# RWKV head pairs: one signal for both heads' copies, weight passes moved from the pairs' fronts into their levels, decay work in other places, and attention's norm sums later

## The chip, the cores and the metric

The kernel runs on one core of one Trainium2 chip. The metric is the device time of one execution in microseconds (us). Before the change it is 2789.9 us, the median of three runs (2789.7, 2789.9 and 2792.98).

## What is computed

A first block (mixers and a feed-forward, not touched here) and then two layers of a hybrid block on 512 tokens of width 1024, all in float32. Each layer is

```
h = rms(x) * g1;  proj = h @ w_in
o_a = sliding_window_attention(rms(q), rms(k), v)     # per head norms
o_b = rwkv7_time_mix(...)                             # 8 heads of 64
o_c = retention(...)
x = x + (g0*o_a@W + g1*o_b@W + g2*o_c@W) @ w_out
x = x + (silu(h2 @ w_gate) * (h2 @ w_up)) @ w_down
```

The RWKV part is the recurrence

```
S = S * w_t + (S a_t) b_t + v_t k_t ;   y_t = S r_t
y = groupnorm(y) * g + b ; y = (y + bonus) * gate
```

with decays `w = exp(-exp(-0.5) * sigmoid(...))`. The kernel computes it in chunks of 64 tokens: inside a chunk a triangular 64x64 system is solved by doubling (one start and five **levels**), and between chunks the state S is carried in eight steps.

## The kernel before, in words

**Weights.** Every large product runs in three passes, since the weights and activations are split into a high and a low half that TensorE takes exactly: `w_hi*xg_hi`, `w_hi*xg_lo`, `w_lo*xg_hi`. One **slot** is one output tile of 128 columns: 8 blocks times 3 = 24 **passes** (128x128 by 128x512) into one of two accumulators, `acc[0]` and `acc[1]`. SyncE loads each slot's raw weights (512 KB) into `raw[s]`; GpSimd rounds them to `w_hi` (line 348, the **high part**) and subtracts to `w_lo` (line 352, the **low part**). GpSimd may write `w_hi[s]` only when pass 16 of the slot before on the same side has been read (`hi_done`), and `w_lo[s]` only after its pass 24 (`slot_done`). VectorE scales a finished accumulator by `rstd` and frees it (`take`).

**A layer's order.** Seven pairs of slots for RWKV; then four **head pairs** j = 0 to 3 (`rwkv_pair`), in which TensorE mixes RWKV's small products with the passes of four slots of the retention projection (96 passes each, given out by `fill(k)`); then three pairs of slots for attention's q, k and v with their norm sums (`head_sums`); then retention and attention themselves among the slots of the output products. The order is written out by hand on every engine: each engine is one queue, and semaphores (`after`, `say`) tie them. `say` on VectorE is a drain and a semaphore increment.

**One head pair** on TensorE: the **front** (32 passes with `variance(j-1)` in between, the `centre` products and transposes after `kh`, 8 passes, then after `ops` the two score products with `eM` and `kp` and transposes, 10 passes), then five levels, each of two **halves**: `X*TL` (32 small products), passes, a wait for `yi` and `gev`, `G*Y` (32 small products), passes, a wait for `xt`. After that the products `au`, `tq`, `dd`, `y0`, and the **tail**, eight state steps that go back and forth with VectorE. VectorE in a half: the two heads p = 0, 1 are copied one after the other (`Y` by an add with the identity, line 1055; `X` by a transpose, line 1626), and each copy is followed by its own `say`:

```
for p in range(2):
    after("y", j, 2 * (lev - 1) + p + 1, 10)
    tt(rw["Y"][:, p], ...)
    say("yi")
```

although TensorE waits for both, and gives both in one increment of 2. VectorE's front: norms, the exponentials' products (`bon`, `kp`, `AR`, `a`, `Dl`, `eM`), then `gated(j-1)` (three operations of the output of the pair before, lines 1535 to 1540), then `say("ops")`, `halves(j-1)` (the split of that output into y1_hi and y1_lo, which says `done`), a take, and the masked scores `SCB`. The next pair's decays are worked into the levels: the scan (line 1514) in level 2 after the transposes, its follow-up in level 3, the key factors in level 5. ScalarE copies G (`swapped`), and in levels 2 to 4 makes the next pair's sigmoids, exponentials and `to_end`. GpSimd masks `TL` (line 440) once a level and does the high and low part of side 0 before level 1 and of side 1 before level 3.

**Attention's norm sums.** TensorE runs `head_sums` of a pair of query tiles between slot 0 and slot 1 of the pair of slots after it, and those of the keys, with four transposes, right after the last slot; it waits there for the squares (line 1690) and then for the roots, before retention's first `rotate`.

## Time and profile before

| | before |
|---|---|
| median of 3 runs | 2789.9 us |
| the profiled execution's own time | 2790.91 us |
| its span, first to last instruction | 2789.1 us |
| mean granted TensorE clock | 0.986 |
| TensorE matmul busy | 94% of the span |
| VectorE, GpSimd, ScalarE busy | 53%, 53%, 23% |
| the two RWKV stretches (four head pairs each) | 786.8 to 1011.7 us and 1828 to 2053 us |

How to read it: the times are of one profiled execution; a matmul's end is modelled, so that a row of passes overlaps the next row a little. In the rows of the timeline the columns are start in us, duration in us, engine, line, operation, output<-inputs, shape and how many instructions were merged; in square brackets stands the idle time of the engine ahead of it and who ended it. PE is TensorE, DVE VectorE, ACT ScalarE, POOL GpSimd.

### The profile page before, as it was taken

Reading aid. Unit: us, or ns where it says so; the run is one execution under the profiler, and the core shown is the slowest. Engines: PE = TensorE matmul, PEld = TensorE weight load, DVE = VectorE, ACT = ScalarE, POOL = GpSimd, SP = SyncE. Lnnn points to the kernel's source line nnn. Section 1 sums busy time; section 2 is a strip of 40 time slices with the busy share of each in tenths; the row PEclk is TensorE's granted clock in tenths of the full one; section 3 lists DMA queues with packets and bytes.
Section 4 is the critical chain, followed back from the end, with each engine's and each line's share of the span. In section 5 each row is a group of like instructions: output and inputs, shape, how many; then the busy total and the mean of one; then the engine's idle time right before and its main releaser. Section 6 shows DMA issues by size and latency. Waiting matters only on the chain.

```text
span 2789.1 us, 47713 instructions
## 1 busy us (share of the span) xinstructions
PE 2634.2 (94%) x16458; PEld 2052.5 (74%) x16458; DVE 1465.7 (53%) x2075; ACT 627.9 (23%) x1143; POOL 1476.9 (53%) x945
## 2 busy tenths in 40 slices
PE   7878999998999899999999999999899989999999
PEld 5656888876766667777788887766667777788887
DVE  5766747364556646773342524456637764442424
ACT  2323000023223313440200002223323440200002
POOL 4554665665544343445666566644444446666665
PEclk9989999999999999999999999999999999999999
DMA  4212333323211121222233333311121223333333
GB/s 145 69 31 78 96 91 97 90 85 101 83 54 47 40 78 57 69 69 81 93 96 92 93 96 111 91 47 49 38 85 57 61 69 90 95 94 92 97 90 98
DMA packets 72727, 222.69 MB, mean 80 GB/s; under 512 B 9344, under 2 KB 12544, under 8 KB 72576
## 3 DMA queue, kind: packets, MB, share of 16 engines
q1 hardware_dynamic: 72576, 220.63, 26.1%
q8 instruction: 100, 1.64, 0.3%
q14 instruction: 51, 0.42, 0.1%
HBM read 218.50 MB, written 2.10 MB: 79 GB/s over the span
## 4 chain that ended last, share of the span: by engine, by line
PE 80%; DVE 10%; issue 4%; DVEq 3%; ACT 1%; DMA 1%; POOL 1%; ACTq 0%; SPq 0%; POOLq 0%
PE acc L464 70%; PE bank L464 8%; DVE rw_X L1626 1%; DVE rw_Y L1055 1%; DVEq L1499 1%; DVE an_mx L1800 1%; DMA raw<-in_w_pg 1%; PE bank L1021 1%; DVE y_lo L1055 0%; DVE an_mx L1055 0%; POOL w_lo L352 0%; DVE rw_SCK L1055 0%; DVE mixed L1055 0%; DVE rw_Dl L1055 0%; DVE an_s L1797 0%
## 5 line engine op out<-in xcount | busy, mean ns | idle before, releaser
L352 POOL TENSOR_TENSOR w_lo<-raw,w_hi 128x1024 fp32r<-128x1024 f32 (+3 forms) x438 | 959.3, 2190 | 300.4 <-PE acc L464 282.8
L348 POOL TENSOR_SCALAR w_hi<-raw 128x1024 fp32r<-128x1024 f32 (+3 forms) x438 | 427.5, 976 | 767.4 <-PE acc L464 645.0
L464 PE MATMUL acc<-xg_hi,w_hi 128*128 128x512 f32 x2224 | 601.9, 407 | 53.4 <-issue 16.0
L464 PE MATMUL acc<-xg_hi,w_lo 128*128 128x512 f32 x2224 | 588.3, 399 | 0.0
L464 PE MATMUL acc<-xg_lo,w_hi 128*128 128x512 f32 x2224 | 587.1, 400 | 0.0
L464 PEld LDWEIGHTS acc<-xg_hi,w_hi 128*128 128x128 f32 x2224 | 416.3, 190 | 174.6 <-issue 80.1
L464 PEld LDWEIGHTS acc<-xg_lo,w_hi 128*128 128x128 f32 x2224 | 419.8, 190 | 102.2 <-issue 1.5
L464 PEld LDWEIGHTS acc<-xg_hi,w_lo 128*128 128x128 f32 x2224 | 417.1, 188 | 101.7 <-issue 1.7
L1845 ACT ACTIVATE ffn_act<-ffn_t 128x512 f32<-128x512 f32 x100 | 63.3, 633 | 812.8 <-DVEq L1115 619.5
L1055 DVE TENSOR_TENSOR x<-x,acc 128x512 f32<-128x512 f32 x104 | 71.3, 688 | 318.4 <-PE acc L464 317.9
L464 PE MATMUL acc<-hid_hi,w_hi 128*128 128x512 f32 x656 | 182.8, 396 | 3.7 <-POOL w_lo L352 1.6
L464 PE MATMUL acc<-hid_hi,w_lo 128*128 128x512 f32 x656 | 182.0, 395 | 0.0
L464 PE MATMUL acc<-hid_lo,w_hi 128*128 128x512 f32 x656 | 181.9, 395 | 0.0
L464 PEld LDWEIGHTS acc<-hid_hi,w_hi 128*128 128x128 f32 x656 | 123.1, 188 | 37.4 <-issue 6.9
L464 PEld LDWEIGHTS acc<-hid_hi,w_lo 128*128 128x128 f32 x656 | 123.2, 188 | 29.9
L464 PEld LDWEIGHTS acc<-hid_lo,w_hi 128*128 128x128 f32 x656 | 123.2, 188 | 29.5
L1055 DVE TENSOR_TENSOR ffn_sq<-acc,rstd 128x512 f32<-128x512 f32 x44 | 30.4, 691 | 212.4 <-PE acc L464 212.4
L1055 DVE TENSOR_TENSOR ffn_t<-acc,rstd 128x512 f32<-128x512 f32 x100 | 69.2, 692 | 136.8 <-PE acc L464 119.4
L1862 ACT ACT_TABLE_LOAD x96 | 123.2, 1283 | 4.6 <-issue 1.7
L440 POOL TENSOR_TENSOR rw_TL<-rw_SCB,lev 128x512 f32<-128x512 f32 x40 | 51.1, 1277 | 97.0 <-DVEq L1499 56.3
L1055 DVE TENSOR_TENSOR ffn_h<-ffn_act,ffn_sq 128x512 f32<-128x512 f32 x44 | 96.0, 2182 | 11.5 <-issue 11.5
L464 PE MATMUL acc<-y_hi,w_hi 128*128 128x512 f32 x256 | 77.9, 427 | 17.9 <-issue 9.9
(342 smaller groups left out, 2738.9 us busy)
## 6 DMA issues: line engine op xcount, KB each, us to landing
raw<-in_w_up SPq DMA_DIRECT2D x132, 512.0 KB, 3.6
raw<-in_w_down SPq DMA_DIRECT2D x48, 512.0 KB, 3.6
raw<-in_w_gate SPq DMA_DIRECT2D x48, 512.0 KB, 3.6
raw<-in_w_ret SPq DMA_DIRECT2D x32, 512.0 KB, 3.6
raw<-in_w_rw SPq DMA_DIRECT2D x28, 512.0 KB, 3.6
raw<-in_w_o SPq DMA_DIRECT2D x48, 256.0 KB, 2.7
raw<-in_w_in SPq DMA_DIRECT2D x18, 512.0 KB, 3.6
raw<-in_w_down SPq DMA_DIRECT2D x24, 384.0 KB, 3.0
```

What stands on the lines that cost most here:

```text
L348: nc.gpsimd.tensor_scalar(w_hi[:, s, 0:n], raw[:, s, 0:n], 1.0, 0.0, ALU.mult, ALU.add).then_inc(w_half[s], 1)
L352: nc.gpsimd.tensor_tensor(w_lo[:, s, 0:n], raw[:, s, 0:n], bits(w_hi[:, s, 0:n]), ALU.subtract).then_inc(w_split[s], 1)
L440: nc.gpsimd.tensor_tensor(rw["TL"][:, lev % 2].rearrange("p h n t -> p (h n) t"), tl, K["lev"][:, lev:lev + 1, :].to_broadcast([P, 8, CH]) ...
L464: return nc.tensor.matmul(o, a, b, start=first, stop=last, skip_group_check=shared)
L1021: last = nc.tensor.transpose(bank[2 * p + j // 2][:, (2 * (j % 2) + b) * P:(2 * (j % 2) + b + 1) * P], an["s"][:, p, j, b * P:(b + 1) * P] ...
L1055: return v.tensor_tensor(o, a, b, op)
L1499: dve.drain()
L1626: v.transpose(rw["X"][:, p].rearrange("p n t -> p (n t)"), bank[3 + p][:, 0:T // 2])
L1800: v.tensor_reduce(an["mx"][:, hs], an["s"][:, p], AX.X, ALU.max)
L1845: return nc.scalar.activation(o, i, f, **kw)
L1862: nc.scalar.preload_act_table_set(name)
```

## The change

1. **One signal for both heads' copies.** In each level VectorE waits once, copies both heads and says `yi` by 2, and the same for `xt`.
2. **Passes.** TensorE's `fill` before `variance` goes from 24 to 14, the next from 8 to 10, the 8 ahead of `ops` go, and the 10 (8 in the last pair) ahead of level 1 become 14. The levels give out 5 per half where they gave 4; `au`, `tq` and the ones behind get one more each.
3. **Front.** `say("ops")` stands ahead of `gated(j-1)`; `gated` writes back to SBUF and says a new `gd`, for which TensorE waits ahead of the AR transposes; the gate product goes to bank 2. The split moves: its high half into level 3, its low half (with `done`) into level 4. `take(0, 0)` moves behind `g1`.
4. **Decays.** The sigmoid is written to SBUF (`eM`) instead of bank 0; the scan reads it there and moves from level 2 to level 5; its follow-up and the last two key steps move behind `auev`; ScalarE's exponentials and `to_end` move behind `keys`. `lora` and the sigmoids go from level 2 to 3, the product `w` from level 1 to 2, the key scores are split around level 1's transposes.
5. **GpSimd.** High and low part of side 0 no longer stand together ahead of level 1: the low part moves ahead of level 3's `TL`, side 1's high part ahead of level 4's, its low part ahead of level 5's.
6. **Attention.** The query sums come a slot pair later, the key sums and transposes inside the first slot of the output stage (after 10 of its passes), retention's value transposes behind that slot; waits for `s4 root` and `s3 z` ahead of them fall away.

The core of the diff:

```diff
 # GpSimd
-                    split_pair((DC, DC), I + 2 * j + 1, range(1))
+                    high_part(0, I + 2 * j + 1, DC * P)
                     for lev in range(1, 6):
                         if lev == 3:
-                            split_pair((DC, DC), I + 2 * j + 1, range(1, 2))
+                            low_part(0, I + 2 * j + 1, DC * P)
+                        elif lev == 4:
+                            high_part(1, I + 2 * j + 1, DC * P)
+                        elif lev == 5:
+                            low_part(1, I + 2 * j + 1, DC * P)
...
 # TensorE, rwkv_pair
-                    fill(24)
+                    fill(14)
                     if j > 0:
                         variance(j - 1)
-                    fill(8)
+                    fill(10)
                     after("kh", j, 1, 1)
...
-                    fill(8)
+                    if j > 0:
+                        after("yroot", j - 1, 1, 1)
                     after("ops", j, 1, 1)
...
                     if j > 0:
-                        after("done", j - 1, 1, 1)
+                        after("gd", j - 1, 1, 1)
...
-                    fill(10 if j < 3 else 8)
+                    fill(14)
...
                         last.then_inc(s2["y"], 2)
-                        if lev == 2 and j < 3:
-                            fill(1)
-                            after("wev", j, 1, 1)
-                            lora(j + 1)
-                        else:
-                            fill(4)
+                        if lev == 2:
+                            fill(3)
+                            after("scev", j, 4, 4)
+                            ...
+                            last.then_inc(s2["w"], 1)
+                        elif lev == 3 and j < 3:
+                            fill(2)
+                            after("wev", j, 1, 1)
+                            lora(j + 1)
+                        else:
+                            fill(5)
+                        after("gev", j, 2 * lev - 1, 11)
                         after("yi", j, 2 * lev, 10)
...
                         last.then_inc(s2["g"], 2)
-                        fill(4)
+                        fill(5)
...
-                    if j < 3:
-                        after("L", j + 1, 1, 1)
...
-                    fill(3 if j < 3 else 2)
+                    fill(4 if j < 3 else 2)
...
-                    fill(1)
+                    fill(2 if j < 3 else 1)
...
-                    fill(3 if j < 3 else 1)
+                    fill(4 if j < 3 else 2)
...
 # TensorE, attention and the output stage
+                slot(0, I, xg, full)
+                slot(1, I, xg, full)
+                variance(3)
+                slot(0, I + 1, xg, full)
+                slot(1, I + 1, xg, full)
+                query_sums(0)
+                slot(0, I + 2, xg, full)
+                after("done", 3, 1, 1)
+                query_sums(1)
+                slot(1, I + 2, xg, full)
...
-                    slot(0, F, xg, full)
+                    if n == 0:
+                        part(0, F, 0, 10)
+                        key_sums()
+                        part(0, F, 10, 24)
+                        values(0)
+                    else:
+                        slot(0, F, xg, full)
...
 # VectorE, rwkv_pair
                     tt(Dl, ra, Dl)
                     tt(eM, ra, eM)
+                    say("ops")
                     if j > 0:
                         gated(j - 1)
-                    say("ops")
-                    if j > 0:
-                        halves(j - 1)
-                    take(0, 0)
...
                     say("g1")
+                    take(0, 0)
                     for lev in range(1, 6):
+                        after("y", j, 2 * lev, 10)
                         for p in range(2):
-                            after("y", j, 2 * (lev - 1) + p + 1, 10)
                             tt(rw["Y"][:, p], ...)
-                            say("yi")
+                        say("yi", 2)
                         if lev == 1:
                             after("sc", j, 2, 2)
+                            key_scores(0)
+                        elif lev == 2:
+                            take(1, 0)
+                        elif lev == 4 and j > 0:
+                            low(j - 1)
+                        elif lev == 5:
+                            take(0, 1)
+                            if j < 3:
+                                decays(j + 1, 1)
+                        if lev < 5:
+                            after("g", j, 2 * lev, 10)
+                            dve.sem_inc(dve_turn, 1)
                             for p in range(2):
+                                v.transpose(rw["X"][:, p]..., bank[3 + p][:, 0:T // 2])
+                            say("xt", 2)
+                        if lev == 1:
+                            key_scores(1)
+                        elif lev == 3 and j > 0:
+                            high(j - 1)
+                        elif lev == 4 and j < 3:
+                            decays(j + 1, 4)
                     after("au", j, 1, 1)
                     v.tensor_copy(rw["AU"][:, 1]..., bank[1][:])
                     say("auev")
+                    if j < 3:
+                        for step in (2, 5, 6):
+                            decays(j + 1, step)
...
 # ScalarE
-                    fn(bank[0][:], bank[0][:], ACT.Sigmoid, bias=vcol(V_W0 + j))
+                    fn(rw["eM"][:], bank[0][:], ACT.Sigmoid, bias=vcol(V_W0 + j))
...
                     if j < 3:
                         keys(j + 1)
+                        exponentials(j + 1)
+                        to_end(j + 1)
```

## Rows read from the trace of the kernel before

**Rows 1.** The page's part 4: the chain that ended last, shares by engine.

```profile
PE 80%; DVE 10%; issue 4%; DVEq 3%; ACT 1%; DMA 1%; POOL 1%; ACTq 0%; SPq 0%; POOLq 0%
```

**Rows 2.** Windows of pair 2 and of attention's slots: stretch, length, busy us by engine.

```profile
900.10:957.50 57.40, 50.92 (x793) 35.91 (x792) 34.98 (x65) 23.64 (x53) 22.26 (x15) 1.00 0.13 38
1011.70:1065.10 53.40, 50.24 (x199) 36.31 (x196) 22.70 (x30) 12.94 (x20) 22.81 (x14) 0.97 0.33 105
```

**Rows 3.** Timeline of pair 1's front in the first layer, from its first pass on.

```profile
842.71 2.10 PE L464 MATMUL acc<-xg_hi,w_hi 128*128 128x512 f32 x8
...
851.96 1.05 PE L464 MATMUL bank<-rw_centre,z_rw 128*128 128x128 f32 x8
...
852.37 0.74 DVE L1535 SCALAR_TENSOR_TENSOR z_rw<-z_rw,vec,rw_Lr 128x512 f32<-128x512 f32 x1
...
855.24 1.10 PE L464 MATMUL bank<-rw_AR,rw_eM 64*64 64x128 f32 x32
...
857.13 1.49 DVE L1055 TENSOR_TENSOR rw_SCB<-bank,rwmask 128x512 f32<-128x512 f32 x2
```

**Rows 4.** Timeline, the same front: two low parts on GpSimd and two VectorE products.

```profile
841.48 2.37 POOL L352 TENSOR_TENSOR w_lo<-raw,w_hi 128x1024 fp32r<-128x1024 f32 x1 [0.17 <-issue]
...
844.08 0.69 DVE L1055 TENSOR_TENSOR rw_bon<-rw_kp,rw_Dl 128x512 f32<-128x512 f32 x1
...
848.81 2.49 POOL L352 TENSOR_TENSOR w_lo<-raw,w_hi 128x1024 fp32r<-128x1024 f32 x1 [0.88 <-PE acc L464]
...
849.14 2.71 DVE L1055 TENSOR_TENSOR rw_Dl<-rw_a,rw_Dl 128x512 f32<-128x512 f32 x1
```

**Rows 5.** Timeline, level 4 of pair 1: two halves, from X*TL to the next X*TL.

```profile
877.39 0.72 PE L464 MATMUL bank<-rw_X,rw_TL 64*64 64x64 f32 x32 [0.35 <-DVEq L1499]
...
878.18 0.42 DVE L1055 TENSOR_TENSOR rw_Y<-bank,ident 128x256 f32<-128x256 f32 x1 [0.96 <-PE bank L464]
...
878.79 0.42 DVE L1055 TENSOR_TENSOR rw_Y<-bank,ident 128x256 f32<-128x256 f32 x1 [0.19 <-issue]
...
879.63 0.69 PE L464 MATMUL bank<-rw_G,rw_Y 64*64 64x64 f32 x32 [0.40 <-DVEq L1499]
...
880.50 0.45 DVE L1626 STREAM_TRANSPOSE rw_X<-bank 128x256 f32<-128x256 f32 x1 [0.40 <-PE bank L464]
...
881.18 0.45 DVE L1626 STREAM_TRANSPOSE rw_X<-bank 128x256 f32<-128x256 f32 x1 [0.23 <-issue]
...
881.81 0.69 PE L464 MATMUL bank<-rw_X,rw_TL 64*64 64x64 f32 x32 [0.36 <-DVEq L1499]
```

**Rows 6.** Timeline, VectorE before level 1: two copies with nothing between them.

```profile
859.58 0.43 DVE L1055 TENSOR_TENSOR rw_G<-bank,ident 128x256 f32<-128x256 f32 x1
...
859.92 0.41 DVE L1055 TENSOR_TENSOR rw_AU<-bank,ident 128x256 f32<-128x256 f32 x1
```

**Rows 7.** Timeline, level 1 and level 2 of pair 1, and the first product behind level 5.

```profile
861.61 0.69 PE L464 MATMUL bank<-rw_X,rw_TL 64*64 64x64 f32 x32 [0.71 <-DVEq L1499]
...
863.59 1.50 DVE L1055 TENSOR_TENSOR rw_SCK<-bank,rwmask 128x512 f32<-128x512 f32 x2 [0.19 <-issue]
...
866.63 0.69 PE L464 MATMUL bank<-rw_X,rw_TL 64*64 64x64 f32 x32 [0.37 <-DVEq L1499]
...
868.19 1.10 PE L464 MATMUL bank<-z_rw,w 128*128 128x512 f32 x2 [0.44 <-ACT rw_AW L1845]
...
870.08 0.70 PE L464 MATMUL bank<-rw_G,rw_Y 64*64 64x64 f32 x32
...
886.18 1.10 PE L464 MATMUL bank<-rw_AW,rw_G 64*64 64x128 f32 x32 [0.34 <-ACT rw_G L1845]
```

**Rows 8.** Timeline, VectorE's wait between `auev` and the first state of pair 1.

```profile
890.91 0.23 DVE L1634 COPY rw_S<-bank 128x64 f32<-128x64 f32 x1 [2.88 <-PE bank L464]
```

**Rows 9.** Timeline, TensorE's wait for `kh` in pair 0's front.

```profile
795.18 1.13 PE L464 MATMUL bank<-rw_centre,z_rw 128*128 128x128 f32 x8 [0.48 <-DVEq L1499]
```

**Rows 10.** TensorE's waits in 1011 to 1066 us: in total, times, longest.

```profile
PE bank L464 <- DVEq L1690: 3.0, 2, 2.2
```

134 lines of the change are left out of this document (58 added, 76 removed).

## The prediction

> **What bounds the kernel now.** I read the page's chain first: 80% of it is TensorE and 10% VectorE [rows 1], so time can only come out of TensorE's idle time or out of its work, and the change removes no TensorE work. Next the windows: in one head pair of 57.4 us TensorE is busy 50.9 us by a count that models matmul ends, in attention's slots 50.2 of 53.4 [rows 2]. The timeline says where the rest goes. In the front, TensorE is nearly full with passes, and VectorE sets when `ops` comes [rows 3]. In the levels TensorE stands in every half with a wait for VectorE [rows 5]. So a pair alternates: a front with too much filling, levels with too little. Below, "pair 1" stands for pairs 1 and 2 of both layers, whose rows repeat within 0.2 us.
>
> **Part 1, one signal for two heads.** With a `say` between them the Y copies start 0.61 us apart, the X copies 0.68 [rows 5]; two copies with nothing between start 0.34 apart [rows 6]. That is 0.27 less per Y (five levels) and 0.34 per X (four). The pause before G*Y is 0.40 and before X*TL 0.36 [rows 5] as modelled; a matmul row ends some 0.16 after its last column is issued (0.40 for one, a spacing of 0.24, from eight passes in 2.10 [rows 3]), so the free time is about 0.55 per half. It now has to hold the saving and one more pass of 0.24: 0.27 + 0.24 and 0.34 + 0.24, that is 0.51 and 0.58 of 0.55. Both sides meet; a level goes from 4.42 [rows 5] to 3.9 (VectorE's limit 3.81, TensorE's about 3.9), and takes ten passes instead of eight. This is the heart of the change.
>
> The Trainium skill (VectorE: DVE Perf Modes, "The DRAIN you can't avoid") says that chained operations flush the pipeline anyway and that semaphores in between cost nothing. By that rule part 1 gives nothing. The trace speaks against it here, 0.34 against 0.61 [rows 5, 6], since a `say` is also a drain of its own; what the rule would make of the time is rival A.
>
> **Level by level.** Level 1 lasted 5.02 (861.61 to 866.63) because both key scores, 1.50 with 0.19 ahead, stood before the transposes [rows 7]; now one fits into the wait for G*Y and one runs beside the next X*TL: 3.9. Level 2 had `lora` (5.63 to level 3); it now has `w` (0.6) and only three passes: 4.0. Level 3 gets `lora`. It waits for ScalarE's `AW` copies: it started 1.56 after X*TL (866.63 to 868.19, with 0.44 of waiting) and G*Y came 1.89 later [rows 7]; as ScalarE's first G copy of 0.38 now also waits for the second transpose, I set 1.95 + 1.9 + 1.9 for the second half = 5.75. Level 3 before was 5.13 since the scan held VectorE; the scan now lies in level 5, where VectorE has no transposes. Level 4: 3.9; the two halves of the split lie in gaps of VectorE in levels 3 and 4 (about 1.0 each, for operations of 0.7), so I cost them at nothing; were the gaps filled, they would cost 0.7 each. Level 5: 4.37 - 0.27 = 4.1. Sum 21.7 against 24.57 (861.61 to 886.18 [rows 7]): **-2.85**. Pair 3 has no lora: 19.85 against 22.66, **-2.8**.
>
> **The front.** TensorE: from 842.71 to the centre products at 851.96 are 32 passes and `variance`, 9.25 us; with 24 passes 1.9 less, so 850.05. The scores came 3.28 after the centre products, with 8 passes and 0.37 of waiting [rows 3]; without them about 1.05, so TensorE can start the scores at 851.1 instead of 855.24. VectorE: `gated` starts at 852.37 and with the waits behind it `ops` comes just before 855.24. Now `ops` stands ahead of `gated`. `Dl` took 2.71 us, since it began 0.33 after a low part on GpSimd and ended 0.55 after it; the same kind of product took 0.69 with GpSimd idle [rows 4]. That low part moves away, which takes 2.0 out of VectorE's chain: `ops` at 850.7. Against that stand two new meetings. GpSimd's last low part waits for pass 96, which moves from the tail's first to its sixth gap: 841.48 becomes about 842.6, ending 845.0, and `bon` at 844.08 then waits for it: +0.8. And the high part of side 0 (it needs pass 16, now behind `variance`) falls onto `AR`, `a` or `Dl`: up to +1.0. With both, the masked scores start at 854.8 instead of 857.13, -2.3; with neither, TensorE binds, 851.1 + the scores and transposes 3.0 + 14 passes 3.3 = 857.4 against 861.61, -4.2. Since the rows show the hold in full where it occurs, I take a value near the first: **-2.6**. `take(0, 0)` behind `g1` lies under X*TL and costs nothing; uncovered it would be 0.7.
>
> Beside the row on `Dl`: the Trainium skill (SBUF — State Buffer, "Who interferes with whom") says that a VectorE operation with two SBUF inputs and a GpSimd one that reads SBUF exclude each other for the whole instruction. The trace agrees, 2.71 against 0.69 [rows 4].
>
> Pair 0 is another case: TensorE already waits 0.48 for `kh` [rows 9], so eight passes fewer there only lengthen that wait. They come back later as 14 for 10: +0.9, less the pause of 0.4 before X*TL and what `Dl`'s cleared road gives (0.3): **+0.15**.
>
> **Behind the levels.** `au` to the tail: three passes more; the first lies in the wait for `auev`, two count: **+0.47** (pair 3: +0.23). The decay steps 2, 5 and 6 are new on VectorE between `auev` and the first state copy: three operations of 0.69 to 0.75, one small one and their drains, 2.9 us; the room is 2.88 [rows 8] and the state's products come 0.24 later. It just fits; nothing. If it does not, each 0.3 over would be 0.3 per pair. ScalarE's exponentials (3.3 us) lie in the tail, where it waits; nothing. The later passes in the tail sit in its gaps. SyncE issues the same loads; side 0's weights are fetched some levels later, but each still has over 10 us before it is split.
>
> **Attention.** TensorE waited 3.0 for the squares [rows 10], and the window leaves 3.2 idle by modelled ends [rows 2]. The upper end from its work: 168 passes at 0.235 (39.5), nine products of 512 float32 columns, each about four such passes' columns (8), eight transposes (0.8), 48.3 of 53.4: 5.1 idle. The sums now come a slot (5.6 us) after their squares, and the roots a half slot. What is late next is the rotation: VectorE needs 5 to 6 us from its last take, TensorE has 24 passes and 3 us of products for it, so little returns. Ends 3.0 and 5.1; I take **-5.0**, near the upper, because every wait gets at least half a slot of cover.
>
> **The sum.** Per layer: pair 0 0.15 - 2.85 + 0.47 = -2.2; pairs 1 and 2 -2.6 - 2.85 + 0.47 = -5.0 each; pair 3 -2.6 - 2.8 + 0.23 = -5.2; attention -5.0: -22.4. Two layers: -44.8. Against the profiled execution's own 2790.91: 2746.1. The median stands 1.0 below it (2789.9), within the spread of the runs shown; I keep **2746**. About 0.2% (5.6 us) can be told from no change here.
>
> **Rivals.**
> A: the drain stays in some form and part 1 gives nothing (the pages' rule). Then 5 * 0.27 + 4 * 0.34 = 2.7 per pair comes back, 21.7 in all: 2767. Against it: rows 6. Chance 0.06.
> B: TensorE becomes the bound in the levels. If each of the 80 halves costs 0.2 more than I count (borders between slots, sequencer waits): +16, 2762. For it: the free time and its new use differ by less than 0.05 a half. Chance 0.14.
> C, on the other side: GpSimd's order. The low part of side 0 (2.4), the high part and the low part of side 1 now stand ahead of the masks of levels 3, 4 and 5, and each waits for a pass before it can run; level n of TensorE waits for its mask. If all three fell onto the path, at most 2.4 each [rows 4], that is 7.2 a pair, 58 in all: 2746 + 58 = 2804, slower. It decides from the point where the mask of level 3 is ready later than 7.9 us after level 1 begins; I count low part and mask done 4 us before that, since pass 24 is long past. Chance 0.04.
> D: the change doesn't do what it says: GpSimd's and VectorE's new meetings and the moved passes give back what the levels win, and TensorE's fixed work shows through: within 0.2% of 2790. Against it: over 6 us of idle time in every pair [rows 2]. Chance 0.04.
>
> **How the numbers follow.** Forecast 0.72, A 0.06, B 0.14, C 0.04, D 0.04. Its own bounds: six fronts at -2.3 to -4.2 (+2, -10), attention 3.0 to 5.1 (+4, 0): 2736 to 2752. The range reaches to B and A at the top: 2736 to 2770. Faster by over 0.2%: 0.92; within: 0.04; slower: 0.04.
>
> **What would show it.** In the profile after: Y and X copies 0.34 to 0.4 apart; X*TL to X*TL 3.9 in level 4; pauses before G*Y below 0.2; `Dl` at 0.7; the masked scores 12 us after the pair's first pass instead of 14.4; level 3 longer than before (5.75), levels 1 and 2 shorter by over 1; `an_sq` waits gone; a head pair of 52.4. I would be wrong if TensorE waits on GpSimd's `TL`, if `yi` pauses stay at 0.4, or if VectorE's first state copy starts late behind the decay steps.

## The result and the profile after

The changed kernel takes 2750.7 us (median of four runs, 2746.3 to 2752.1) against 2789.8 for the kernel before (four runs, 2789.4 to 2793.0): a ratio of 0.9855, with an interval of 0.9838 to 0.9872. The forecast was 2746, from 2736 to 2770. The profiled execution has its own time of 2751.0 and a span of 2749.2, which is 39.9 us less than the one before; the forecast against that execution was 44.8 less. The wanted effect came, about 5 us smaller than counted.

The page of the changed kernel, parts 1 and 4 (busy time and instructions of each engine; the chain that ended last):

```profile
PE 2628.6 (96%) x16458; PEld 2049.6 (75%) x16458; DVE 1458.3 (53%) x2075; ACT 627.9 (23%) x1143; POOL 1479.6 (54%) x945
...
PE 85%; DVE 8%; DVEq 3%; issue 3%; DMA 1%; POOL 1%; ACT 0%; ACTq 0%; SPq 0%; POOLq 0%
```

TensorE's share of the chain went from 80% [rows 1] to 85%, and it is busy for 96% of a shorter span. No TensorE work was taken out, so this is mostly idle time that closed; the busy time itself fell from 2634.2 to 2628.6 us, which the clock in attention explains for the larger part. The windows of pair 1 (from its first pass to the next pair's) and of attention's slots (from the first slot to retention's first score product, which stands behind `rotate` and the first slot of the output stage) say where:

```profile
841.36:894.05 52.69, 50.77 (x793) 35.62 (x793) 33.56 (x65) 23.64 (x53) 22.75 (x15) 1.00 0.14 40
996.06:1044.61 48.55, 48.02 (x197) 35.82 (x195) 22.48 (x30) 10.94 (x18) 24.17 (x15) 1.00 0.37 116
```

A pair has the same 793 matmuls and nearly the same busy time by the modelled count (50.8 us, pair 2 before had 50.9), in 52.7 us instead of 57.4 [rows 2]; attention has 48.0 busy in 48.6 instead of 50.2 in 53.4. There the same products also took 2.2 us less of busy time, since the granted clock of the stretch is 1.00 where it was 0.97 [rows 2]: in the kernel before, the keys' norm sums behind the wait of 2.2 us, their transposes and `rotate` ran at a mean clock of 0.61 (1054 to 1058 us), and from the start of the sums to that of the transposes stood 1.84 us, where 0.86 stand now. TensorE's waits between pair 1's first level and its end were these before (5.0 us in ten waits on VectorE), and are these after:

```profile
PE bank L464 <- DVEq L1499: 5.0, 10, 1.1
PE bank L464 <- ACT rw_AW L1845: 0.4, 1, 0.4
```

```profile
PE bank L475 <- ACT rw_AW L1886: 0.5, 1, 0.5
PE bank L475 <- PE bank L475: 0.4, 1, 0.4
PE bank L475 <- DVEq L1526: 0.3, 1, 0.3
```

What is left is one wait for ScalarE in level 3, one for TensorE's own product, and one for VectorE. The timeline of a level shows the same from inside (level 4 of pair 1, the counterpart of [rows 5]):

```profile
871.46 0.69 PE L475 MATMUL bank<-rw_X,rw_TL 64*64 64x64 f32 x32
...
872.22 0.76 DVE L1082 TENSOR_TENSOR rw_Y<-bank,ident 128x256 f32<-128x256 f32 x2 [0.55 <-PE bank L475]
...
873.45 0.69 PE L475 MATMUL bank<-rw_G,rw_Y 64*64 64x64 f32 x32
...
874.32 0.84 DVE L1659 STREAM_TRANSPOSE rw_X<-bank 128x256 f32<-128x256 f32 x2 [0.53 <-PE bank L475]
...
875.43 0.69 PE L475 MATMUL bank<-rw_X,rw_TL 64*64 64x64 f32 x32
```

The two heads' copies now stand in one row ("x2"), 0.76 us for both Y copies where the rows before had two that started 0.61 apart. Neither product of TensorE has a wait shown beside it any more. The halves are 1.99 and 1.98 us, with five passes in each: a level of 3.97 where it was 4.42.

### The profile page after: what moved, and what is told of

It reads as the page before. It is cut to its first block, busy times and chain, and to the rows that moved or that the text cites. A ratio compares the mean times of both kernels' runs of the same rounds, so it can differ in the third digit from the quotient of the medians.

```text
span 2749.2 us, 47579 instructions
## 1 busy us (share of the span) xinstructions
PE 2628.6 (96%) x16458; PEld 2049.6 (75%) x16458; DVE 1458.3 (53%) x2075; ACT 627.9 (23%) x1143; POOL 1479.6 (54%) x945
## 4 chain that ended last, share of the span: by engine, by line
PE 85%; DVE 8%; DVEq 3%; issue 3%; DMA 1%; POOL 1%; ACT 0%; ACTq 0%; SPq 0%; POOLq 0%
PE acc L475 75%; PE bank L475 9%; DVE an_mx L1841 1%; DMA raw<-in_w_pg 1%; PE bank L1048 1%; DVEq L1526 0%; DVE an_mx L1082 0%; POOL w_lo L354 0%; DVE mixed L1082 0%; DVE an_s L1838 0%; DVE rw_bon L1082 0%; DVE z_rw L1082 0%; DVEq L1840 0%; DVEq L1616 0%; DVE y_lo L1082 0%
## 5 line engine op out<-in xcount | busy, mean ns | idle before, releaser
L457 POOL TENSOR_TENSOR x<-x,z_rt 128x1024 f32<-128x1024 f32 x8 | 19.0, 2371 | 131.0 <-DVEq L1526 131.0
```

The lines of the kernel that those rows point to most:

```text
L457: nc.gpsimd.tensor_tensor(x[:, 2 * j:2 * j + 2, :], x[:, 2 * j:2 * j + 2, :], z_rt[:, 15:16, :].to_broadcast([P, 2, T]), ALU.mult)
```

## Where the time came from, stretch by stretch

Read from the timelines of the two kernels, first layer, in us (the second layer repeats it within 0.2 us a piece, but for two places told below). "Front" goes from the first pass of a pair to its first `X*TL`, "levels" from there to the product `au`, "behind" from `au` to the next pair's first pass.

| | before | after | difference | forecast |
|---|---|---|---|---|
| front, pair 1 | 18.90 | 16.31 | -2.59 | -2.6 |
| levels, pair 1 | 24.57 | 21.91 | -2.66 | -2.85 |
| behind, pair 1 | 13.92 | 14.47 | +0.55 | +0.47 |
| levels, pair 3 | 22.66 | 20.23 | -2.43 | -2.8 |
| attention, first slot to retention's first scores | 53.39 | 48.55 | -4.84 | -5.0 |
| pair 0, `centre` to `X*TL` | 9.06 | 9.30 | +0.24 | +0.15 |

Summed over the stretch from pair 0's `centre` products to retention's first scores the first layer went from 269.91 to 249.03 (-20.9) and the second from 269.78 to 250.56 (-19.2), where -22.4 each was forecast. The 40.1 us of the two stretches are the whole difference of the spans.

## Experiments

Each was timed beside the kernel before (medians of 2789.8 to 2792.2 in the four groups of runs). Ratios are to that kernel; the segments come from the timelines. The changed kernel's 2750.7 comes from another group than the runs below, and its own two medians lie 1.9 apart; so a difference of medians between two edited kernels holds to some 2 us, and the segments are the finer measure.

### The changed kernel again

No edit.

> The changed kernel once more, unaltered, as the base for the runs beside it. Both theories: 2746 to 2752 us, X*TL to X*TL 3.97 us in level 4, level 1 to the product behind level 5 21.9 us in pair 1 of the first layer. If the 1.2 us by which pair 1 of the second layer ran longer in the first trace (a pause of 0.92 inside one row of 32 products, put down to issue) is a matter of the single run, it is gone or elsewhere here.

Measured: 2752.64 us (2747.85 to 2755.77), ratio 0.986 [0.9843, 0.9876]. The changed kernel repeats, within the spread that the kernel before shows too (4 to 9 us within one group of runs).

### The attention part alone

The kernel before with TensorE's new order of the norm sums, key sums and value transposes, and nothing else:

```diff
+                slot(0, I + 1, xg, full)
+                slot(1, I + 1, xg, full)
+                query_sums(0)
...
+                    if n == 0:
+                        part(0, F, 0, 10)
+                        key_sums()
+                        part(0, F, 10, 24)
+                        values(0)
```

> The kernel before with attention's part of the change alone (query sums a slot pair later, key sums inside the first output slot, retention's value transposes behind it). Theory: the stretch from attention's first slot to retention's first scores goes from 53.4 to 48.5 us per layer, 9.8 us in all, 2780. Rival (the waits only move on to retention's rotation): less than 4 us, 2786 or more.

Measured: 2780.48, ratio 0.9962 [0.9948, 0.9976], 11.7 us less than the 2792.18 beside it. The last segment (from pair 3's first state product to retention's first scores) went from 59.30 to 54.44 in the first layer, -4.86, as in the changed kernel; no other segment got shorter by more than 0.15. In the second layer it is 55.98, because there the first passes behind pair 3's tail ran at a mean clock of 0.66. The part is independent of the rest and worth what the change as a whole shows for it. Its 4.86 are the two waits of 3.0 in all, less the 0.5 that is left, and some 2.3 us by which the products behind the second wait had run longer than at full clock. TensorE's remaining waits in this stretch of the changed kernel are these two of 0.5 us, for VectorE's rotation and for the last state:

```profile
PE bank L475 <- DVEq L1759: 0.5, 1, 0.5
PE bank L475 <- DVEq L1526: 0.5, 1, 0.5
```

### One signal alone, on the kernel before

```diff
+                        after("y", j, 2 * lev, 10)
                         for p in range(2):
-                            after("y", j, 2 * (lev - 1) + p + 1, 10)
                             tt(rw["Y"][:, p], ...)
-                            say("yi")
+                        say("yi", 2)
```

and the same for `xt`; four passes in a half as before.

> The kernel before with the single signal for both heads alone, nothing else moved. Theory: each half shortens by 0.27 or 0.31 except the one that lora fills and with 0.3 lost to ScalarE's later start ahead of lora: 2.0 to 2.6 us per pair, 16 to 19 us in all (2771 to 2774); a level goes from 4.42 to 3.85, TensorE still waits 0.1 per half. Rival (the signal is worth nothing): 2790, a level stays at 4.42.

Measured: 2774.53, ratio 0.9938 [0.9922, 0.9955], 16.3 us less than before. The halves went from 2.24 and 2.18 to 1.93 and 1.82, that is by 0.31 and 0.36, against 0.27 and 0.34 predicted. Rival A, that the signal between two copies costs nothing, is out: of the two parts that were tried on the kernel before it is the larger.

### Two signals again, on the changed kernel

```diff
                             tt(rw["Y"][:, p], ...)
-                        say("yi", 2)
+                            say("yi")
...
                                 v.transpose(rw["X"][:, p]...)
-                            say("xt", 2)
+                                say("xt")
```

VectorE's single wait ahead of both copies stays.

> The changed kernel, but VectorE drains and signals after each head again (yi and xt). Theory (the drain between the heads costs 0.27 to 0.34 of start to start, and the halves have no room for it once each holds five passes): Y copies 0.61 and X copies 0.68 apart again, halves 2.24 and 2.18 instead of 1.99 and 1.98, 1.6 to 1.9 us per pair, +13 to +15 us in all (2763 to 2766). Rival (signals between chained operations cost nothing, the passes did it all): 0, halves stay 1.98.

Measured: 2756.86, ratio 0.9875 [0.9859, 0.9892], 4 to 6 us above the changed kernel where 13 to 15 were expected. **A miss**, and the most useful run of the study. The halves of level 4 are 1.99 and 2.07: the Y half did not move at all. Level 5's Y copies in this kernel:

```profile
876.43 0.97 DVE L1082 TENSOR_TENSOR rw_Y<-bank,ident 128x256 f32<-128x256 f32 x2 [0.15 <-PE bank L475]
```

0.97 for both means that the second started 0.55 after the first (each takes 0.42), not 0.61; so the signal between them is back. Yet `G*Y`, at 877.65, came no later. Either VectorE's path was never as close to TensorE's as I had counted, or something else in the change had shortened it. Two more things did change in this place: VectorE waits once instead of twice, and TensorE waits for `gev` ahead of `yi`, where it had waited for `yi` first. The next two runs take these.

The segments give this run less than its median: the levels of all eight pairs are 2.1 us longer in all. In level 3 of pairs 0 to 2 they are even shorter, 5.52 for 5.69, since ScalarE can copy the first head's G before the second is transposed: its `AW` copies start 0.76 behind `X*TL` instead of 1.01. The profiled execution also has four pauses without a cause (told at the end), 3.8 us in all, where the changed kernel's has one.

### The first part wholly undone

The changed kernel with two signals, two waits, and TensorE's waits in the old order:

```diff
-                        after("gev", j, 2 * lev - 1, 11)
                         after("yi", j, 2 * lev, 10)
+                        after("gev", j, 2 * lev - 1, 11)
...
-                        after("y", j, 2 * lev, 10)
                         for p in range(2):
+                            after("y", j, 2 * (lev - 1) + p + 1, 10)
                             tt(rw["Y"][:, p], ...)
-                        say("yi", 2)
+                            say("yi")
...
```

and the same for `xt`.

> The changed kernel with its first part wholly undone: VectorE waits for each head's product and signals each head's copy, and TensorE waits for the copies of Y before those of G, as before the change; all moved work and the ten passes of a level stay. The run with two signals but one wait and the new order of TensorE's waits had cost only 4 us (halves 2.07 and 1.99 us). Theory: the size I had predicted for the first part (0.27 per Y, 0.34 per X) is right for the whole of it, and what that run kept (one wait on VectorE, G's copies waited for first on TensorE) carried the rest. Then the halves are about 2.24 and 2.18 us, a level 4.4, and the kernel about 13 to 15 us above the changed one, 2764 to 2767. Rival: with five passes in a half TensorE is the bound and the two waits lie beside them; then it stays 3 to 5 us above the changed one, 2754 to 2756.

Measured: 2765.65, ratio 0.991 [0.9893, 0.9927], 14.9 us above the changed kernel. The halves of level 4 are 2.21 and 2.17, the old ones, although five passes stand in each; the levels of pair 3 went from 20.23 to 21.98, those of the others by 1.3 to 1.6. Its rows:

```profile
872.87 0.42 DVE L1082 TENSOR_TENSOR rw_Y<-bank,ident 128x256 f32<-128x256 f32 x1 [0.38 <-PE bank L475]
...
873.48 0.42 DVE L1082 TENSOR_TENSOR rw_Y<-bank,ident 128x256 f32<-128x256 f32 x1 [0.19 <-issue]
...
874.33 0.69 PE L475 MATMUL bank<-rw_G,rw_Y 64*64 64x64 f32 x32
```

Copies 0.61 apart, and `G*Y` starts 0.43 after the last copy's end; in the changed kernel's rows above it starts 0.47 after it, but there TensorE's own passes hold it. So VectorE's path is again the longer one, and the first part is worth 12 us (the levels' segments of the eight pairs) to 15 us (the medians) in the changed kernel, of which the signals alone give 2 to 6.

### The order of TensorE's two waits

The run with one signal on the kernel before, and in it:

```diff
+                        after("gev", j, 2 * lev - 1, 11)
                         after("yi", j, 2 * lev, 10)
-                        after("gev", j, 2 * lev - 1, 11)
```

> The kernel before with one signal and one wait for the two heads' copies (as in the run of the signal alone, ratio 0.9938, halves 1.93 for Y and 1.82 for X), and now TensorE also waits for G's copies before those of Y, as the changed kernel does. Everything else as before, four passes in a half. Theory: with the old order TensorE reads its second semaphore only after VectorE's copy of Y and so starts G*Y later; with the new one the Y half falls to the 1.75 us of the run with four passes. Four Y halves of each of eight pairs times 0.18 make 5 to 6 us less than the signal alone: ratio about 0.992. Rival: the order of the two waits is nothing and the halves of that other run were shorter through the moved work; then the ratio stays at 0.9938.

Measured: 2771.29, ratio 0.993 [0.9913, 0.9948], 3.2 us less than with the signal alone; the medians' intervals overlap, but the rows don't leave a doubt. Level 4 of pair 1 with the signal alone, then with the order too:

```profile
874.58 0.69 PE L464 MATMUL bank<-rw_X,rw_TL 64*64 64x64 f32 x32
...
875.33 0.76 DVE L1055 TENSOR_TENSOR rw_Y<-bank,ident 128x256 f32<-128x256 f32 x2 [0.93 <-PE bank L464]
...
876.51 0.69 PE L464 MATMUL bank<-rw_G,rw_Y 64*64 64x64 f32 x32
```

```profile
873.70 0.69 PE L464 MATMUL bank<-rw_X,rw_TL 64*64 64x64 f32 x32
...
874.45 0.76 DVE L1055 TENSOR_TENSOR rw_Y<-bank,ident 128x256 f32<-128x256 f32 x2 [0.93 <-PE bank L464]
...
875.45 0.69 PE L464 MATMUL bank<-rw_G,rw_Y 64*64 64x64 f32 x32
```

The copies start 0.75 after `X*TL` in both and take 0.76 in both. `G*Y` starts 0.42 after their end in the first and 0.24 in the second. ScalarE's copies of G, for which `gev` stands, end 0.36 ahead of VectorE's in both. So the wait that is already fulfilled costs TensorE 0.18 when it is read after the late one and is off the path when it is read before it. The half fell to 1.75 as expected. The sum was expected at 5 to 6 and came to 3, since in levels 1 to 3 other work sets the end (the key scores, ScalarE's copies behind `lora`, the scan): the levels' segments of the four pairs and two layers add up to 3.3 us less.

Here every piece has its size. Between the starts of two Y copies lie 0.34 with nothing between, 0.55 with a signal, 0.61 with a signal and a wait; for X copies 0.33 to 0.39, 0.57 and 0.69. The order of TensorE's waits is 0.18 more per Y half. VectorE's path in a half is about 1.75 (Y) and 1.83 to 1.90 (X) with one signal, TensorE's with five passes 1.98: so two signals bring VectorE's path to about 1.96 (1.75 + 0.21) for Y and the measured 2.07 for X, hardly over TensorE's 1.98. That explains the miss.

### Four passes in a half

The changed kernel with the two passes of a level moved back behind the scores:

```diff
-                    fill(14)
+                    fill(22 if j < 3 else 23)
...
-                            fill(5)
+                            fill(4)
...
-                        fill(5)
+                        fill(4)
```

> The changed kernel with four passes per half of a level instead of five, the eight (nine in pair 3) passes put back ahead of level 1. Theory (the passes in the levels lie almost wholly in VectorE's time): halves go from 1.99 and 1.98 to VectorE's own 1.97 and 1.87, so a pair wins 0.5 in the levels and pays 1.9 less 0.3 in the front: +1.1 to +1.4 per pair, +9 to +11 us in all. Rival (TensorE binds in the levels, so a pass costs 0.23 wherever it stands): halves 1.75, the sum unchanged within 2 us.

Measured: 2757.73, ratio 0.9885 [0.9869, 0.9902], about 7 above the changed kernel's 2750.7 and 5 above the 2752.6 of its second measurement, between the two theories. The segments are sharper: the front from the scores to `X*TL` grew from 6.84 to 8.38, the levels fell from 21.91 to 20.81, net +0.44 in pair 1; over the eight pairs some 4 us. Its profiled execution has besides four pauses of 0.6 to 1.1 us without a cause (told at the end), 3.5 in all, where the changed kernel's has one of 0.9. With four passes the halves of level 4 are 1.75 and 1.90 (1.83 in levels 1 to 3), VectorE's path. A pass costs 0.19 in the front (1.54 for eight) and 0.14 in the levels (1.10 for eight); so moving the eight passes into the levels gains only about half a microsecond a pair.

### GpSimd's order

```diff
                     high_part(0, I + 2 * j + 1, DC * P)
+                    low_part(0, I + 2 * j + 1, DC * P)
                     for lev in range(1, 6):
                         if lev == 3:
-                            low_part(0, I + 2 * j + 1, DC * P)
-                        elif lev == 4:
                             high_part(1, I + 2 * j + 1, DC * P)
-                        elif lev == 5:
                             low_part(1, I + 2 * j + 1, DC * P)
```

> The changed kernel with GpSimd's order of before: low part of side 0 straight behind its high part, side 1's parts together ahead of level 3's mask. Theory (two VectorE inputs in SBUF and a GpSimd operation exclude each other, and ops is on the path in the front): the low part runs from about 849.1 to 851.5 in pair 1, Dl takes 2.5 instead of 0.69, ops and level 1 come 1.8 to 2.0 later in pairs 1 to 3, +10 to +12 us in all. Rival (the mask order is what matters, or nothing): within 2 us of the changed kernel.

Measured: 2763.72, ratio 0.9903 [0.9886, 0.9919], 13 above the changed kernel. The scores come 4.10 behind the centre products instead of 2.03 in every pair but the first. The rows of this kernel's front:

```profile
849.08 2.35 POOL L354 TENSOR_TENSOR w_lo<-raw,w_hi 128x1024 fp32r<-128x1024 f32 x1 [0.47 <-PE acc L473]
849.22 2.76 DVE L1080 TENSOR_TENSOR rw_Dl<-rw_a,rw_Dl 128x512 f32<-128x512 f32 x1
...
852.76 1.10 PE L473 MATMUL bank<-rw_AR,rw_eM 64*64 64x128 f32 x32 [2.60 <-DVEq L1524]
```

`Dl` is at 2.76 again and TensorE waits 2.60 for it. Six pairs by 2.07 are 12.4, nearly the whole loss. TensorE stands still for 2.60 us at these six places, and the granted clock stays at 1.00 behind each of them.

### `ops` behind the gated product, and the same with the pause filled

```diff
-                    say("ops")
                     if j > 0:
                         gated(j - 1)
+                    say("ops")
```

> The changed kernel with the signal ops behind the three operations of gated, as before. Theory (TensorE waits for ops in pairs 1 to 3 already 0.5 us): scores 2.4 later, level 1 about 2.1 later in those pairs, +12 to +13 us in all. Rival (VectorE's masked scores set level 1, and they wait for gated either way): the scores 2.4 later but level 1 only about 1.2 later, +7 us.

Measured: 2771.53, ratio 0.9923 [0.9904, 0.9942], 20.8 above the changed kernel, outside both theories. The delay itself is as counted (scores 4.37 behind the centre products, 2.34 more than 2.03), but behind it the piece up to `X*TL` is 9.36, 7.98 and 6.52 us in pairs 1 to 3, where 6.84 stood. The timeline and the windows of that place (busy us of TensorE, its weight load, VectorE, ScalarE and GpSimd, then the granted clock, the DMA share and GB/s):

```profile
852.96 1.98 PE L475 MATMUL bank<-rw_AR,rw_eM 64*64 64x128 f32 x32 [2.88 <-DVEq L1526]
854.87 1.11 PE L801 MATMUL bank<-ident,rw_Dl 128*128 128x128 f32 x4
...
855.91 1.99 PE L475 MATMUL bank<-rw_AR,rw_kp 64*64 64x128 f32 x32
```

```profile
847.00:850.00 3.00, 3.00 (x20) 2.53 (x18) 2.92 (x4) 0.09 (x1) 1.45 (x1) 1.00 0.00 0
850.00:853.00 3.00, 0.12 (x5) 0.07 (x5) 2.54 (x4) 1.08 (x2) 0.00 (x0) 0.90 0.00 0
853.00:859.00 6.00, 6.00 (x73) 5.00 (x74) 3.60 (x8) 0.00 (x0) 2.03 (x2) 0.50 0.01 3
859.00:862.00 3.00, 3.00 (x14) 2.36 (x13) 0.76 (x2) 2.84 (x8) 2.65 (x2) 0.96 0.00 0
```

After a wait of 2.88 us the granted clock is 0.50 of 2.4 GHz, that is 1.2 GHz, for 6 us, and the row of 32 products takes 1.98 instead of 1.10. Pair 2 does the same (0.73 in the 6 us from its scores on), pair 3 doesn't: behind 2.86 us its clock is 1.00 and its row takes 1.10. The second layer repeats all three. I took the clock for the cause of the extra and tested it: the same edit, with eight of the fourteen passes behind the scores put ahead of the wait.

```diff
                     if j > 0:
+                        fill(8)
                         after("yroot", j - 1, 1, 1)
...
-                    fill(14)
+                    fill(6 if j > 0 else 14)
```

> The changed kernel with ops behind the gated product, as before the change (in pairs 1 to 3, as in the run that cost 20.8 us), but now with eight of the fourteen passes that stand behind the scores put back ahead of the wait for ops, so that TensorE has no pause of 2.9 us there. Theory: that pause alone made the granted clock fall to half, and the fall carried what that run lost beyond the delay itself. Then the clock stays at 1.00 in the front, the scores come 4.4 us after the centre products, X*TL about 5.7 after them, and the kernel is 6 to 9 us above the changed one, 2757 to 2760. Rival: the fall has another cause or VectorE's lateness is the cost; then X*TL stays 8 to 9 us behind the scores and the kernel near 2771.

Measured: 2756.71, ratio 0.9875 [0.9859, 0.9892]: 6.0 above the changed kernel, and 14.8 below the same delay without passes in it. VectorE is exactly as late (scores +4.35), `X*TL` follows 5.57 behind, and the clock stays:

```profile
852.46 1.10 PE L475 MATMUL bank<-rw_AR,rw_eM 64*64 64x128 f32 x32 [1.00 <-DVEq L1527]
```

```profile
850.00:853.00 3.00, 2.00 (x27) 1.41 (x29) 2.05 (x3) 0.81 (x2) 0.00 (x0) 1.00 0.00 0
853.00:859.00 6.00, 5.15 (x103) 3.93 (x93) 4.58 (x10) 2.92 (x8) 3.05 (x3) 1.00 0.01 3
```

So moving `say("ops")` is worth 6 us with the cover of the passes and 21 without it, and the change, which took that cover away, depends on it. The 14.8 between the two are not all clock. From the centre products to `X*TL` pair 3 of the uncovered run, whose clock didn't fall, takes 2.0 more than in the changed kernel, and six such pairs would make 12.1, the theory's number; pairs 1 and 2 lose 2.8 and 1.4 beyond that, 8.4 in both layers, with the clock. In the covered run each of the six pairs takes 1.05 to 1.19 more. So about 8.4 of the 14.8 are the clock, and 5.6 are the passes that now stand in the wait.

### A version that beats both

Three leftovers were seen in the profile after: `bon` at 1.48 us, since GpSimd's last low part of a pair starts a gap late; pair 0's `kh`, for which TensorE waits 2.35; and in its second layer a clock below 1.00.

```diff
-                    fill(10)
+                    fill(10 if j > 0 else 18)
...
-                    fill(14)
+                    fill(14 if j > 0 else 6)
...
-                    fill(4 if j < 3 else 2)
+                    fill(5 if j < 3 else 2)
```

> The changed kernel, with one more pass ahead of y0, so that pass 96 lies in the first gap of the tail again (pairs 0 to 2), and in pair 0 18 passes ahead of kh and 6 ahead of level 1 instead of 10 and 14. Theory: GpSimd's last low part ends before bon, bon takes 0.69 instead of 1.48, TensorE's waits for ops (0.54) and ahead of level 1 (0.26) go, less 0.23 for the pass: -0.5 in six pairs; pair 0's wait of 2.35 for kh shrinks to 0.5 and level 1 comes 0.8 earlier, twice: -4 to -5 us against the changed kernel in the same call, 2745. Rival (the next meeting with GpSimd's high part takes its place): bon is short but a, Dl or eM longer, less than 2 us.

Measured: 2742.01 (2741.5 to 2744.7), ratio 0.9824 [0.9808, 0.984], 8.7 below the changed kernel and faster than both. In pairs 1 to 3 the scores come 1.42 behind the centre products instead of 2.03 and `X*TL` 6.52 behind instead of 6.84, while the part behind the levels gives back 0.14 to 0.27; pair 0's piece fell from 6.52 to 5.57, in the second layer from 6.82, with the clock at 1.00. `bon` is at 0.69 as expected. The rival is there too, at a lower price: GpSimd's high part now meets `Dl`, which takes 1.38, instead of `a`, which took 1.53. The stretches from pair 0's `centre` products to retention's first scores account for 6.0 us of the gain. The rest lies ahead of them, in a part that the edit doesn't touch: pair 0's `centre` products stand at 793.1 us instead of 795.6. In the next version they stand at 793.3, in the two profiled executions of the changed kernel and in its six other edits between 794.0 and 795.6; whether that is scatter isn't shown.

One more step filled what was left: four passes ahead of `ops` in pair 0 (out of its levels 4 and 5), and one moved under ScalarE's wait in level 3.

```diff
+                    else:
+                        fill(4)
...
-                            fill(2)
+                            fill(3)
                             after("wev", j, 1, 1)
```

> The version that beat both kernels (pass 96 early, pair 0's passes spread), with passes moved once more: in pair 0 four of them before the wait for ops, taken from its levels 4 and 5, and in level 3 of the other pairs one moved from the second half into the first, under the wait for ScalarE. Theory: the pauses that are left there (about 1.2 us in pair 0, 0.5 in level 3) are filled with work that otherwise stands in halves that TensorE binds; 2 to 3 us less than that version, 2739 to 2740, ratio 0.9815. Rival: the other halves then wait for VectorE instead and nothing is won, 2742.

Measured: 2741.86 (2739.2 to 2742.6), ratio 0.9822 [0.9806, 0.9839]. The segments show the expected gain (pair 0's levels 21.91 to 21.13, the others' 21.92 to 21.78, 2.1 us in all for both layers), but the medians, 2742.0 and 2741.9, can't tell the two versions apart. Inconclusive for the time.

## Why the prediction held, and where it was off

**What bounds the kernel.** Right in the main: the time came out of TensorE's idle time in the fronts, the levels and attention. It had one more source, which I had not seen: in attention TensorE's own products ran faster, as their clock no longer fell.

**Part 1.** The saving was right in the sum it was used for and its mechanism incomplete. I put 0.27 and 0.34 down to the `say` between two copies. It is 0.21 for the signal and 0.06 to 0.12 for the second wait, plus 0.18 on TensorE for the order of its waits, which the diff shows and which I did not cost at all. It came out right in the levels because TensorE is the bound there: I had put "TensorE's about 3.9" for a level, the rows have 3.97. That term of the sum was mis-sized, by 0.03 to 0.04 in every half. It is rival B's mechanism at a sixth of its price. VectorE's limit was off by more, and it did no harm: 3.81 for a level predicted, 3.58 to 3.65 measured with four passes, since I had left out the order of the waits. So "both sides meet" was wrong: VectorE had some 0.3 us of room in a level. The level came out near 3.9 because TensorE's limit stood there for itself; that VectorE's, counted wrongly, lay beside it is luck. Rival A fell with the runs: had the part given nothing, 21.7 us were to come back; undone whole it gave back 14.9. It can't give back 21.7, since the five passes hold the half at 1.98 anyway. The rule of the Trainium skill that I set against it (VectorE: DVE Perf Modes, "The DRAIN you can't avoid": a chain of copies takes as long with a semaphore after each as with one at the end) is not what these rows show for copies of 256 columns with an explicit drain ahead of each signal, 0.55 against 0.34.

**Level by level.** Level 1 lasts 3.97 (3.9 predicted), level 2 4.13 (4.0), level 3 5.69 (5.75), level 4 3.97 (3.9), level 5 4.15 (4.1): 21.91 against 21.7 predicted. No level is off by more than 0.15, and four of five are longer than I had them: that is TensorE's limit again. Level 3 is set by ScalarE as foreseen, with this wait in its middle:

```profile
867.58 1.10 PE L475 MATMUL bank<-z_rw,w 128*128 128x512 f32 x2 [0.45 <-ACT rw_AW L1886]
```

**The front.** Right in its sum and in both meetings that I added. In the timeline of pair 1's front, the counterpart of [rows 3, 4]:

```profile
841.25 2.40 POOL L354 TENSOR_TENSOR w_lo<-raw,w_hi 128x1024 fp32r<-128x1024 f32 x1 [1.57 <-PE acc L475]
...
842.72 1.48 DVE L1082 TENSOR_TENSOR rw_bon<-rw_kp,rw_Dl 128x512 f32<-128x512 f32 x1
...
847.28 1.47 POOL L347 TENSOR_SCALAR w_hi<-raw 128x1024 fp32r<-128x1024 f32 x1 [3.63 <-PE acc L475]
847.76 1.53 DVE L1082 TENSOR_TENSOR rw_a<-rw_a,rw_kk 128x512 f32<-128x512 f32 x1
848.80 1.05 PE L475 MATMUL bank<-rw_centre,z_rw 128*128 128x128 f32 x8
849.36 0.69 DVE L1082 TENSOR_TENSOR rw_Dl<-rw_a,rw_Dl 128x512 f32<-128x512 f32 x1
...
850.83 1.10 PE L475 MATMUL bank<-rw_AR,rw_eM 64*64 64x128 f32 x32 [0.54 <-DVEq L1526]
...
853.42 1.50 DVE L1082 TENSOR_TENSOR rw_SCB<-bank,rwmask 128x512 f32<-128x512 f32 x2 [0.19 <-issue]
```

`Dl` fell to 0.69; `bon` rose by 0.79 (0.8 predicted) behind the last low part, and `a` by 0.84 behind the high part (up to 1.0 predicted). The masked scores start 12.06 after the pair's first pass, 12 predicted, 14.42 before. That -2.6 came out to 0.01 is luck: I had placed it between two ends, -2.3 and -4.2, by a judgement on how fully the two meetings would hold. Both tensor inputs of these VectorE operations are in SBUF; the Trainium skill (SBUF — State Buffer, "Who interferes with whom") says that such an operation and one of GpSimd that reads SBUF exclude each other, and both the low part's subtract and the high part's multiply agree here.

**Behind the levels.** VectorE's new decay steps fit: it still waits 0.69 for the first state, of the 2.88 before [rows 8]:

```profile
884.67 0.23 DVE L1674 COPY rw_S<-bank 128x64 f32<-128x64 f32 x1 [0.69 <-PE bank L475]
```

The passes there cost 0.55 in pair 1, 0.47 predicted, and up to 0.72 in the other pairs 0 to 2.

**Attention.** -4.84 for -5.0. The waits for the squares are gone, and retention's first scores are held for 0.53 only, by VectorE's rotation. I had two counts of the idle time, 3.0 to 3.2 from waits and windows and 5.1 from the work at full speed, took a value near the second and gave the cover of the waits as the reason. The rows give another reason for the 2 us between the counts: they are the products that ran at the lower clock behind the wait. So the number was right and the reason for it missing.

**Pair 0.** The front is +0.24 for +0.15; and the wait for `kh` grew from 0.48 [rows 9] to 2.35, with a second of 1.22 behind it. I had costed this at nothing beyond the eight passes' place. In the first layer it was nothing; in the second the clock fell on it, which took 0.3 in the profiled run and up to 2.4 in others (`X*TL` 8.92 to 8.97 behind the scores in three profiled runs instead of 6.52).

**The 5 us in the sum.** By the segments, for both layers: the levels 1.9 (0.8 and 1.1; 0.1 to 0.2 in each of pairs 0 to 2, 0.4 in pair 3), the parts behind the levels 0.9 besides the pause, attention 0.3, and the clock in pair 0 of the second layer 0.3. Behind the levels of pair 1 in the second layer 15.87 us stand instead of the first layer's 14.47, that is 1.4 more, 0.92 of them a pause that no semaphore ended. These make 4.8, of which 0.2 come back in the other fronts; 4.7 were to be found.

**Rivals.** B is what was seen, at 2 to 3 us instead of 16. A, C and D didn't come: GpSimd's masks never held TensorE, and no wait in the levels names them.

## What to carry to other kernels

When two engines take turns in a loop, write down both paths of a half turn. Here they are 1.75 to 1.9 (VectorE) and 1.98 (TensorE with five passes): on the shorter one a signal more costs 2 to 6 us over the whole kernel; in the kernel before, where VectorE's path was the longer one, the signal and its wait cost 16. Put the wait that comes last at the end of a list of waits. And when you take filling work off an engine that will then wait, ask how long it will wait and look at the granted clock behind it: here the same delay cost 6 us with passes in it and 21 without, 8.4 of them through the clock. And where a busy count of unchanged work shrinks, look at the clock of that stretch before crediting the new order of the work.

## What the runs showed that I had not expected

**The granted clock after a pause.** Windows of the changed kernel in pair 0 of the second layer, where TensorE waits 2.35 for `kh`, and of the version with eight passes put into them:

```profile
1808.00:1813.00 5.00, 5.00 (x22) 3.78 (x21) 4.45 (x7) 1.16 (x2) 3.27 (x2) 1.00 0.33 75
1813.00:1818.00 5.00, 2.65 (x13) 2.46 (x12) 4.73 (x8) 0.00 (x0) 0.00 (x0) 0.76 0.08 32
1818.00:1823.00 5.00, 5.00 (x80) 4.03 (x79) 3.00 (x7) 2.04 (x5) 1.29 (x1) 0.90 0.00 0
```

```profile
1808.00:1813.00 5.00, 3.29 (x38) 2.54 (x40) 4.04 (x7) 1.08 (x2) 0.00 (x0) 1.00 0.00 0
1813.00:1818.00 5.00, 4.20 (x69) 3.08 (x61) 3.76 (x9) 1.92 (x6) 2.38 (x2) 1.00 0.02 3
1818.00:1823.00 5.00, 4.94 (x107) 3.72 (x108) 3.72 (x8) 3.09 (x6) 4.34 (x4) 1.00 0.13 25
```

The first layer of the same run has the same wait and a clock of 1.00. That repeats: eight profiled executions (the changed kernel twice, and six of its edits) have the wait of 2.35 in pair 0 of both layers. In all eight the clock falls below 1.00 behind it in the second layer, in none in the first; only the depth differs, from 0.3 to 2.4 us lost. With 2.88 us it fell in pairs 1 and 2 of both layers and in pair 3 of neither, and with 2.60 us (GpSimd's old order) at none of six places. So the length of the pause alone doesn't decide it; the place does as well, and which property of the place isn't shown. The two versions that fill the wait have 1.00 in both layers.

The same fall stands at two more places. Behind pair 3's tail, in the first passes of attention, it took 1.1 to 1.6 us in one layer of five of the fourteen profiled executions (the changed kernel's second measurement, two signals, attention alone, and the two runs of the signal on the kernel before). In the run of the signal alone it also stands at attention's keys in both layers: the four products of `rotate` run at 0.50 and take 3.75 us, 1.88 in the changed kernel. That is why the last segment of that run is 61.1 and 62.7 us instead of 59.3.

**Pauses without a cause.** In one row of 32 small products (`tokV`, `tokK`, behind the levels) a pause of 0.37 to 1.40 us stands now and then, and no semaphore ends it. It is in five of the fourteen profiled executions: one pause in the changed kernel's and in the early version's, four each with two signals, with four passes and with the first part undone. It always stands in pair 1 behind the 13th product or in pair 3 behind the 10th. So it is bound to a place of the program and not spread at random; what causes it stays open.
